# A softmax reciprocal two steps ahead, and value pages on four column groups of TensorE

## The reference, cut to what matters

```python
def block(args):                       # prompt: 4 blocks of 128 queries
    s = jnp.einsum('bqhd,bkhd->bhqk', qi, k) * scale
    s = s + ci.transpose(0, 2, 1)[..., None] - cum_k
    s = jnp.where(kpos[None, :] <= pi[:, None], s, -jnp.inf)
    p = jax.nn.softmax(s, axis=-1)
    return jnp.einsum('bhqk,bkhd->bqhd', p.astype(v.dtype), v)
...
# sample: scores s_p against the pages kp, s_n against the row's own key
p = jax.nn.softmax(jnp.concatenate([s_p, s_n], axis=-1), axis=-1)
o = (jnp.einsum('bhqk,bkhd->bqhd', p[..., :P].astype(v.dtype), vp)
     + jnp.einsum('bhqk,bkhd->bqhd', p[..., P:].astype(v.dtype), v))
```

## Time and profile before

| | |
|---|---|
| median of 3 runs | 1976.04 us (1971.9 to 1979.23) |
| profiled execution: time, span | 1975.2 us, 1973.4 us |
| mean granted clock of TensorE | 0.931 |
| PE, DVE, ACT, POOL busy | 92%, 44%, 29%, 11% of the span |
| chain that ended last, by engine | PE 80%, POOL 6%, DVE 5%, issue 4% |

### The profile page before, as it was taken

How to read it: one execution, slowest core, us unless ns; L and a number is a source line. 1 busy time by engine, 2 the same in 40 slices (tenths; PEclk the granted TensorE clock), 3 DMA queues, 4 the chain that set the end, 5 groups by cost and what they waited for, 6 DMA issues and landing times.

```text
span 1973.4 us, 31959 instructions
## 1 busy us (share of the span) xinstructions
PE 1810.4 (92%) x12929; PEld 1557.9 (79%) x12929; DVE 867.8 (44%) x1461; ACT 576.0 (29%) x816; POOL 214.0 (11%) x228
## 2 busy tenths in 40 slices
PE   5899878869989999999899999999977899999997
PEld 3899433322979999999797879889836799999997
DVE  2599345530453322322542736526545533323324
ACT  2322432200243222212332433423332342222122
POOL 1000046620110000000100110100220100000001
PEclk8899666669999999999899999999997999999998
DMA  8473044457542552552232443622653133323221
GB/s 285 142 213 95 3 133 117 117 159 246 181 150 86 172 168 87 171 161 76 73 102 75 149 156 103 202 75 86 216 197 112 47 96 96 96 86 96 80 83 52
DMA packets 288066, 248.82 MB, mean 126 GB/s; under 512 B 9000, under 2 KB 239816, under 8 KB 287951
## 3 DMA queue, kind: packets, MB, share of 16 engines
q1 hardware_dynamic: 262740, 173.97, 30.0%
q0 software_dynamic: 15824, 58.99, 8.7%
q10 hardware_dynamic: 9395, 14.36, 2.2%
HBM read 224.05 MB, written 23.70 MB: 126 GB/s over the span
## 4 chain that ended last, share of the span: by engine, by line
PE 80%; POOL 6%; DVE 5%; issue 4%; DMA 2%; ACT 2%; ACTq 0%; POOLq 0%; DVEq 0%
PE product L726 58%; PE product L741 6%; POOL prod L2116 4%; PE product L966 3%; PE job L1131 2%; PE job L623 2%; PE job L1114 1%; POOL sqa L2083 1%; PE job L617 1%; DMA bfg<-in_b_forget 1%; PE job L656 1%; PE job L1106 1%; PE job L1017 1%; PE job L1037 1%; PE job L844 1%
## 5 line engine op out<-in xcount | busy, mean ns | idle before, releaser
L726 PE MATMUL product<-H_hi,w_lo 128*128 128x260 f32 x2368 | 674.2, 285 | 3.0 <-ACT gate L1163 2.9
L726 PE MATMUL product<-H_lo,w_hi 128*128 128x260 f32 x2368 | 669.1, 283 | 0.0
L726 PE MATMUL product<-H_hi,w_hi 128*128 128x260 f32 x2368 | 668.5, 282 | 0.0
L726 PEld LDWEIGHTS product<-H_hi,w_lo 128*128 128x128 f32 x2368 | 445.9, 188 | 16.2 <-issue 14.2
L726 PEld LDWEIGHTS product<-H_hi,w_hi 128*128 128x128 f32 x2368 | 446.5, 189 | 0.0
L726 PEld LDWEIGHTS product<-H_lo,w_hi 128*128 128x128 f32 x2368 | 446.2, 188 | 0.2
L1552 DVE TENSOR_TENSOR w_lo<-raw,w_hi 128x1024 fp32r<-128x1024 f32 (+1 forms) x228 | 275.2, 1208 | 166.3 <-ACT w_hi L1163 165.6
L1163 ACT ACTIVATE w_hi<-raw 128x1024 fp32r<-128x1024 f32 (+1 forms) x228 | 234.7, 1037 | 320.7 <-PE product L726 188.2
L726 PE MATMUL product<-G_hi,w_lo 128*128 128x260 f32 x912 | 260.8, 286 | 5.9 <-DVE X L1636 2.5
L726 PE MATMUL product<-G_lo,w_hi 128*128 128x260 f32 x912 | 259.8, 285 | 0.0
L726 PE MATMUL product<-G_hi,w_hi 128*128 128x260 f32 x912 | 259.7, 285 | 0.0
(11 more groups left out here) (318 smaller groups left out, 2166.3 us busy)
## 6 DMA issues: line engine op xcount, KB each, us to landing
spare<-in_ada_w POOLq DMA_DIRECT2D x24, 1024.0 KB, 9.3
raw<-in_w_in_odd SPq DMA_DIRECT2D x48, 512.0 KB, 3.9
raw<-in_w_ffn_gate SPq DMA_DIRECT2D x44, 512.0 KB, 4.1
raw<-in_w_ffn_up SPq DMA_DIRECT2D x44, 512.0 KB, 3.9
kp<-in_cache_k SPq DMA_DIRECT2D x64, 256.0 KB, 2.7
raw<-in_w_ffn_down SPq DMA_DIRECT2D x32, 512.0 KB, 3.8
st<-in_state_ret POOLq DMA_DIRECT2D x28, 512.0 KB, 4.7
out_ret_sample<-st POOLq DMA_DIRECT2D x28, 512.0 KB, 4.9
```

What stands on the lines that cost most here:

```text
L726: mm = pe.matmul(Gp[slot][:, c, 0:CH], w[:, j, k, :], x[:, k, cols], start=k == 0 and p == 0, stop=k == kt - 1 and p == 2)
```

## The change

It has two parts. In the score loop DVE takes the reciprocal `inverse(x+2)` where it took `inverse(x+1)`, with one more before the loop; POOL's list stays. In the value stage the weights of a page become 32 columns at a step of 16 (the 8 heads of the right sample and page at every fourth column, others between them), and page `g` goes to the column group `g % 4`, so that two pages are accumulated in each of four groups of 32 PSUM rows. `SC` gets a ninth head of zeros, which the last column reads; the mask `own_head`, the product `vm` and `gather` have 128 rows where they had 8.

```diff
-    SC = sb("SC", [P, HEADS, NB, 8])
+    SCP = sb("SC", [P, HEADS + 1, NB, 8])
+    SC = SCP[:, 0:HEADS]
...
-    vm = sb("vm", [HEADS, 2, 512])
+    vm = sb("vm", [P, 2, 512])
...
+            def weights_of(b, g):
+                first = b * PAGES + g
+                return SCP[:].rearrange("p h b g -> p (h b g)")[:, first:first + 31 * 16 + 1:16]
+
             def gather(b):
                 pe.wait_ge(vm_ready, b + 1)
                 for t in range(4):
                     mm = pe.matmul(turned[:, t * NB + b:t * NB + b + 1], vm[:, b % 2, t * P:(t + 1) * P],
-                                   one_col[0:HEADS], start=True, stop=True)
+                                   one_col, start=True, stop=True)
...
                     pe.wait_ge(v_page[g], 16 * (b + 1))
-                    mm = pe.matmul(Gp[b // 2 % 2][0:HEADS, b % 2, :], SC[:, :, b, g], vp[:, g, :],
-                                   start=g == 0, stop=g == 7)
+                    rows = slice(QD * (g % 4), QD * (g % 4) + QD)
+                    mm = pe.matmul(Gp[b // 2 % 2][rows, b % 2, :],
+                                   weights_of(b, g), vp[:, g, :],
+                                   start=g < 4, stop=g >= 4)
                     mm.then_inc(v_used, 1)
...
             inverse(0)
+            inverse(1)
             for h in range(HEADS):
                 for q in range(TB):
                     x = h * TB + q
-                    if x + 1 < HEADS * TB:
-                        inverse(x + 1)
+                    if x + 2 < HEADS * TB:
+                        inverse(x + 2)
...
-            own_head = con[0:HEADS, C_ID:C_ID + HEADS].unsqueeze(2).broadcast_to((HEADS, HEADS, HD))
+            own_head = con[:, C_OWN:C_OWN + HEADS].unsqueeze(2).broadcast_to((P, HEADS, HD))
...
                 n.up(v.tensor_tensor(vm[:, b % 2, :].rearrange("p (h d) -> p h d", d=HD),
-                                     Gp[b // 2 % 2][0:HEADS, b % 2, :].rearrange("p (h d) -> p h d", d=HD),
+                                     Gp[b // 2 % 2][:, b % 2, :].rearrange("p (h d) -> p h d", d=HD),
                                      own_head, ALU.mult), vm_ready)
...
             v = nc.gpsimd
             n = Tally(pool)
+            v.memset(SCP[:, HEADS], 0.0)
...
+        c[QD * q:QD * q + QD:QD // HEADS, C_OWN:C_OWN + HEADS] = np.eye(HEADS)
```

More of the change, by code:

```diff
@@ L50 @@
 C_ALL = C_SUM + 16
-C_END = C_ALL + 10
+C_OWN = C_ALL + 10
+C_END = C_OWN + HEADS
 QD = 32
```

## The result

The change makes the kernel faster: 1930.76 us (median of 4 runs, 1925.21 to 1931.06) against 1977.63 us (median of 4 runs of the kernel before beside them, 1971.9 to 1981.4), a ratio of 0.9759 with a 95% interval of 0.9728 to 0.9789. The forecast was 1940, with a range of 1924 to 1957.

The account below looks back on a forecast made before the run. POOL's wait for DVE's reciprocal was taken to bound the score loop, and PE's products the value stage, with page loads next. 1975.2 us less 27 less 9 is 1939; with 0.8 us up to the median, 1940, range 1924 to 1957.

Parts of the forecast that it names:

- the case named likeliest: Whole kernel: both parts pay, 1940 us (1928 to 1950), chance 0.60.
- The reciprocal's size: Score loop: heads fall from 17.83 to 14.4 us over 7.75 heads, 27 us saved (20 to 37).
- what PE is busy with today, at today's mixture of clocks: Score loop: PE's busy time per head, 14.4 us, taken as a head's length after the change.
- PE nearly full: Score loop, sign to look for: a head lasts about 14.4 us with PE busy nearly throughout.
- The better bound: Score loop: PE's clock rises and POOL alone counts, 13 us a head, 37 us saved.
- The column groups: 9 us: Value stage: last `vm` begins 10.7 us earlier, less 2 us for the clock, 9 us left.
- the 2 us taken off: End of value stage: last gather and first `out_even` products run at the lower clock, costing 2 us.
- the page's price: Value stage: DMA bytes pace pages, 0.82 us each at 318 GB/s, taken as 0.86 us.
- The bound of 0.67 us: Value stage: a page at the 394 GB/s other 2 KB-row loads reached, which gives 18 us.
- the rival with 0.22: Value stage gives nothing: PE waits between short bursts, clock falls, 8.2 us a sample; 1949 us, chance 0.22.
- The loop's wait: Score loop rival: POOL waits for DVE's sums instead, only heads' ends won, 9 us for 27; 1958 us, chance 0.10.
- the other two: Whole-kernel rivals: neither part gives anything, 1974 us, chance 0.05; slower, column groups not overlapping, 2011 us, chance 0.03.

Follow-up runs that it names:

- the reciprocal alone: Kernel before with only the reciprocal taken two steps ahead, value stage as before: 1941.19 us, ratio 0.9823.
- the filler: Kernel after with one useless 512-column PE product behind each block's scores in the loop: 1924.24 us, ratio 0.974; the same added to the kernel before: 1970.08 us.
- the deeper ring: Kernel after with a ring of 16 value pages for 8, the first sixteen asked for early by SP: 1915.75 us, ratio 0.9699.
- half pages: Kernel after with pages of samples 1 to 7 loading only 256 of 512 columns: 1920.92 us, ratio 0.9718.
- two groups: Kernel after with value pages in two column groups in place of four: 1931.16 us, ratio 0.9757.
- the first eight early: Kernel after, ring of eight kept, SP asking early for all eight pages of the first sample: 1930.23 us, ratio 0.9761.
- the late low part: Kernel after with ACT copying the head's output aside and DVE making its low part two steps later: 1936.47 us, ratio 0.9799.
- the column groups alone: Kernel after with the reciprocal's lines as before, so only the value stage changed: 1964.65 us, ratio 0.9944.
- without the early requests: Kernel after with a ring of 16, first eight pages asked for as in the kernel after, second eight only behind these: 1919.7 us, ratio 0.9706.

## Why the prediction was right, point by point

Direction, range and the case named likeliest held, the time near that case's fast end. In spans the sum was 36 us and the profile shows 50.0; the difference of 14.0 is 4.9 in the loop, 2.3 in the value stage, and 2.3, 2.4 and 2.1 in three places that the sum did not have. The median of the runs lies 5.6 above the profiled one, so that in medians 46.9 us stand against 36.

**The reciprocal's mechanism is shown.** POOL's wait fell from 43.2 to 1.4 us and came back in small part before its products, as forecast; the reciprocal alone gives the whole of it, and a higher clock without it doesn't. Costing the moved instruction at nothing was right: between 264 and 374 us DVE's reciprocal stands in no wait of the kernel after, so its sums were always ready.

**The reciprocal's size was off: 27 us against 31.9.** The term that was mis-sized is "what PE is busy with today, at today's mixture of clocks", 14.4 us a head. Over the same five heads as in the earlier trace rows (291.36 to 360.54) a head took 13.84, and the two and a quarter heads ahead of them gained 10.3 us where 7.7 were reckoned. The mixture is no constant: as the holes went, the clock rose from 0.62 to 0.73 and PE was busy 17 us less for the same columns. "PE nearly full" failed with it: PE is busy 0.85 of the loop, POOL with its two waits is the loop. The better bound, 13 us a head with POOL alone, is where the filler brought it (12.80).

**The column groups: 9 us against 11.3.** The page was put at 0.86 us; over the 55 pages that were waited for it took 46.0 us (398.64 to 444.65), 0.836 each, 1.3 us less in all. The first of them landed 6.1 us behind the first product rather than 5.4. And the 2 us taken off "for the clock, which I expect to be down for part of the stage" were not due: it was down in the first sample alone, as it was before the change. That 9 came near 11.3 is partly luck, for these errors have both signs.

**The reason for the page's price failed.** "At 283 GB/s for a share of 0.89, a full share would move 318 GB/s" treats the DMA engines as the limit. In the middle of the stage they moved 305 GB/s, near that, but half the bytes took 0.742 us a page, and 16 slots carried 404 to 406 GB/s. The limit is a slot's way round: 8 slots in about 6.7 us. The bound of 0.67 us that was named, from other loads, is what the deeper ring reached (0.647). The number came out near by a route that doesn't hold; the phrase "the ring of eight and two queues won't keep every DMA engine fed" was the cause, treated as a correction.

**The rivals.** The value stage gave its gain, against the rival with 0.22. The state that it feared, short bursts with waits and a lower clock, is half there: the bursts and waits of 0.74 and 1.28 us are, the clock is 1.00. The Trainium skill, "TensorE: Matmul & The Clock Gate", section "HAM oscillation — how this bites in real kernels", describes a loop whose waits for DMA are longer than its bursts of products; here the waits, at most 1.40 us in the kernel after, are not. The prediction carried the section over to waits that it doesn't describe, and this trace neither bears it out nor speaks against it. The rival's lower clock can occur in this stage: it was 0.50 for a stretch with half pages (410.5 to 417.0 us), two groups (418.5 to 421.5) and the first eight early (442.5 to 445.5), just after waits of 2.33, 1.83 and 1.29 us. In the late low part a wait of 2.14 us left it at 1.00, so no rule comes out of these.

The loop's wait did move, to the products, but with 10.1 us of 43.2 rather than all those inside heads. The price of that rival, 9 us at 1.2 us a head, stands on no row and was too low for what it describes. Of POOL's 30 holes the 22 of 0.89 us inside heads hold 19.6 us and the seven at heads' ends 22.4, so winning the ends alone would have been worth up to 22. Nothing of the other two was seen.

**What was not in the sum.** The chain of short steps lasted 18.7 to 19.3 us in nine of the fourteen profiles and 21.1 to 21.9 in the other five, on both sides of the change (21.1 with the column groups alone and with the early ring of 16, 18.7 without the early requests). The two lengths go with the clock: 0.65 to 0.71 in the nine, 0.57 to 0.59 in the five. PE has the same 37 records in it before and after, and is busy for 10.92 us in the one (408.00 to 429.15) and 8.55 in the other (373.80 to 392.56), which is the whole 2.4 us. Since either length comes on both sides, they are not put down to the change. The loop's start (262.0 to 268.9 us over the profiles) and the 2.1 us behind `out_even`, where the other profiles lie between 1473.9 and 1477.5, also differ from profile to profile, with no cause shown.

## What to carry to other kernels

When an engine waits for a tiny instruction of another, look at what is queued ahead of that instruction, not at its duration: 0.15 us of reciprocal cost 32 us of a loop of 142, clock included, because it stood behind sums that needed the waiting engine's last product. For a stream through a ring, work out a slot's whole way round (issue, landing, use) before a bandwidth: if that time over the number of slots is the pace, another slot is worth more than faster use or fewer bytes. And do not carry an engine's busy time at a mixed clock over a change that closes its holes, for the clock can change with it, as it did here.

## What the runs showed of the hardware

- Additional products that nobody reads raised the granted clock of the loop from 0.73 to 0.98 and shortened it from 110.0 to 100.0 us.
- Short bursts with waits such as those of 0.74 and 1.28 us between them left the clock at 1.00 over 51.10 us with PE busy for 40.38. In three other profiles of this stage it fell to 0.50 for a stretch, after waits of 1.29 to 2.33 us.
- A DVE product with both inputs in SBUF took 1.70 to 1.82 us beside POOL's products and made two of these take 2.94 to 2.96 us for 2.49; with one input in PSUM it took 0.68 or 0.69.
- One core moved 404 to 406 GB/s of 2 KB rows for 20 us, with the time to landing at 5.5 us. The Trainium skill, "HBM Reference", section "Specifications (TRN2)", gives some 425 GB/s for a core that streams alone and 358 when both of a pair do; the measured 405 lies near the former, and no run here has a second core at work.
